# A two-block transformer kernel on one core: the transposed x is split piece by piece at the stage boundaries

## The reference, cut to what matters

```
x = x + 0.5 * swiglu(rmsnorm(x, g), w_in, w_out)     # eight of these, d_ff 2816
x = x + mixer(rmsnorm(x, g), ...)                     # hgrn, forgetting attention (fox), short conv, sparse attention (nsa)
kv = projection of rmsnorm(x, kv_norm)                # keys and values for nsa

rmsnorm(x, g) = x * rsqrt(mean(x*x) + 1e-6) * g
swiglu(h, w_in, w_out) = (silu(h @ w_in[gate]) * (h @ w_in[up])) @ w_out
```

## Time and profile before

| | us |
|---|---|
| median of 3 runs | 2198.05 |
| lowest, highest | 2197.47, 2202.11 |
| the profiled execution | 2199.34 |
| its span, first to last instruction | 2197.9 |
| TensorE busy | 2122.4 |
| VectorE busy | 1202.0 |
| ScalarE busy | 1009.3 |
| mean granted clock of TensorE | 0.988 |

### The profile page before, as it was taken

The page is one execution under the profiler, slowest core; times in us unless marked ns, Lnnn a source line. Parts: engine busy times, 40 slices in busy tenths (PEclk is TensorE's granted clock), DMA queues, the critical chain, the costliest instruction groups (busy, mean ns, idle before and its releaser), DMA issues.

```text
span 2197.9 us, 25948 instructions
## 1 busy us (share of the span) xinstructions
PE 2122.4 (97%) x10523; PEld 1756.2 (80%) x10523; DVE 1202.0 (55%) x1458; ACT 1009.3 (46%) x1272; POOL 25.6 (1%) x49
## 2 busy tenths in 40 slices
PE   8998999999999999999999999899999999998999
PEld 6887987888888776788888879788876887787887
DVE  6445686554545564654465556555555445765444
ACT  6344435444544454553454343444445344764342
POOL 1000000000000000000000000000000000000000
PEclk9999999999999999999999999999999999979999
DMA  8553425565555441455555535675635754213553
GB/s 262 192 172 116 153 96 173 194 204 194 196 173 194 132 154 58 144 194 196 174 173 192 196 129 175 188 225 172 199 107 127 236 173 156 98 39 133 193 173 115
DMA packets 265379, 361.01 MB, mean 164 GB/s; under 512 B 19856, under 2 KB 206652, under 8 KB 265133
## 3 DMA queue, kind: packets, MB, share of 16 engines
q1 hardware_dynamic: 256800, 351.57, 48.4%
q10 hardware_dynamic: 7772, 7.17, 1.9%
q0 software_dynamic: 688, 0.62, 0.1%
HBM read 357.75 MB, written 1.57 MB: 163 GB/s over the span
## 4 chain that ended last, share of the span: by engine, by line
PE 90%; DVE 6%; ACT 3%; issue 1%; ACTq 1%; DMA 0%; POOL 0%; SPq 0%; DVEq 0%
PE bank L388 18%; PE bank L390 17%; PE bank L389 17%; PE acc L648 6%; PE acc L649 6%; PE acc L650 6%; PE bank L383 2%; PE bank L385 2%; PE bank L384 2%; PE tr L628 2%; PE acc L678 1%; PE acc L680 1%; PE acc L679 1%; PE tr L471 1%; DVE x_tok L774 1%
## 5 line engine op out<-in xcount | busy, mean ns | idle before, releaser
L388 PE MATMUL bank<-w_hi_,xt_hi_ 128*128 128x512 f32 x1760 | 708.0, 402 | 12.1 <-DVE h_tok L753 4.9
L412 DVE TENSOR_TENSOR w_lo_<-raw_in,w_hi_ 128x2048 fp32r<-128x2048 f32 (+1 forms) x327 | 572.4, 1759 | 225.1 <-ACT w_hi_ L402 224.8
L390 PE MATMUL bank<-w_hi_,xt_lo_ 128*128 128x512 f32 x1760 | 689.3, 392 | 0.0
L389 PE MATMUL bank<-w_lo_,xt_hi_ 128*128 128x512 f32 x1760 | 687.9, 391 | 0.0
L402 ACT ACTIVATE w_hi_<-raw_in 128x2048 fp32r<-128x2048 f32 (+1 forms) x327 | 480.0, 1483 | 78.4 <-PE bank L390 22.8
L758 DVE TENSOR_TENSOR wo_lo_<-raw_out,wo_hi_ 128x2048 fp32r<-128x2048 f32 x80 | 183.4, 2292 | 478.8 <-ACT wo_hi_ L724 478.8
L388 PEld LDWEIGHTS bank<-w_hi_,xt_hi_ 128*128 128x128 f32 x1760 | 332.3, 189 | 82.6 <-issue 6.6
L390 PEld LDWEIGHTS bank<-w_hi_,xt_lo_ 128*128 128x128 f32 x1760 | 331.5, 188 | 71.5
L389 PEld LDWEIGHTS bank<-w_lo_,xt_hi_ 128*128 128x128 f32 x1760 | 332.7, 189 | 62.7
L724 ACT ACTIVATE wo_hi_<-raw_out 128x2048 fp32r<-128x2048 f32 x80 | 153.3, 1916 | 365.1 <-PE acc L650 358.0
L648 PE MATMUL acc<-wo_hi_,ht_hi_ 128*128 128x512 f32 x576 | 224.2, 389 | 0.0
(11 more groups left out here) (314 smaller groups left out, 1825.4 us busy)
## 6 DMA issues: line engine op xcount, KB each, us to landing
raw_in<-ffn_w_in SPq DMA_DIRECT2D x352, 512.0 KB, 4.9
raw_out<-ffn_w_out SPq DMA_DIRECT2D x88, 1024.0 KB, 4.9
raw_in<-hg_w_in SPq DMA_DIRECT2D x16, 1024.0 KB, 5.1
raw_in<-fox_w_in SPq DMA_DIRECT2D x16, 1024.0 KB, 5.4
raw_in<-conv_w_in SPq DMA_DIRECT2D x12, 1024.0 KB, 5.2
raw_in<-hg_w_out SPq DMA_DIRECT2D x4, 1024.0 KB, 5.0
raw_in<-fox_w_out SPq DMA_DIRECT2D x4, 1024.0 KB, 5.1
raw_in<-conv_w_out SPq DMA_DIRECT2D x4, 1024.0 KB, 5.2
```

The costliest lines, as they stand in the source:

```text
L388: mm(o, g.xt_hi_[:, k, tok], wh[:, par, k, 0:w], start=first, stop=False)
L389: mm(o, g.xt_hi_[:, k, tok], wl[:, par, k, 0:w], start=False, stop=False)
L390: last = mm(o, g.xt_lo_[:, k, tok], wh[:, par, k, 0:w], start=False, stop=end)
L412: dve.e.tensor_tensor(g.piece(g.wl, n, half, k), raw, g.piece(g.wh, n, half, k).bitcast(F32), ALU.subtract).then_inc(g.w_lo, 4 if k is Non ...
```

## The change

The turn of x is changed in all thirteen stages. The gains product into `g.xg` and the semaphore `scaled` are gone. ScalarE reads a 128x128 piece of the transposed x from PSUM and applies the gains as its scale; VectorE computes piece * gain - high part in one instruction, from the same piece in PSUM. Each stage has 16 such pieces on each engine in place of four halves (ScalarE) and four plus four (VectorE). Tile 1 is turned into banks of its own, two of the accumulators, and k alternates between the two banks of a tile. ScalarE waits for VectorE's piece k-2 before it reads piece k, so that the two never read one bank together. `xt_lo` and `xt_hi` now count pieces, and the product waits for each k. hgrn, conv and kv (`BY_K`) take the pieces in the order k, then tile; the others tile, then k. In mixer stages both diagonals are made before the first piece. In FFN stages the squares, the roots and 1/rms move from the turn of x to the `between` place of chunk 0.

The routines that turn other operands (`pe_turn_o` and its like) keep their instructions; only their counts change. Two waits are added in stages 8 and 10, where small matmuls use a bank that the turn of x now uses.

```diff
+BY_K = (S_HGRN, S_CONV, S_KV)
...
+def turn_order(s):
+    if s in BY_K:
+        return [(t, k) for k in range(KT) for t in range(NT)]
+    return [(t, k) for t in range(NT) for k in range(KT)]
...
+def pieces_for(u, t, k, feature_major, both):
+    if both:
+        return 8 * (k // 4) + 8
+    if u not in U:
+        return 8 * t + 4 * (k // 4) + 4
+    if U.index(u) in BY_K:
+        return 2 * k + (2 if feature_major else t + 1)
+    return 8 * (1 if feature_major else t) + k + 1
...
-            if f == 0 and k % 4 == 0:
-                operands(k // 4)
+            if f == 0:
+                operands(k)
...
+def x_turned(g, s, t, k):
+    a = 2 if s == S_FFN[7] else 0
+    bank = (g.tr[0], g.tr[1], g.accs[a], g.accs[a + 1])[2 * t + k % 2]
+    return bank[:, k // 2 * P:(k // 2 + 1) * P]
...
 def pe_turn_x(g, pe, s):
-            if t:
-                pe.wait_ge(g.scaled, 4 * s + half + 1)
             pe_wait_x(g, pe, s, t, half)
...
+def act_norm(g, act, s):
+    for t in range(NT):
+        act_squares(g, act, s, t)
+    for t in range(NT):
+        act_root(g, act, s, t)
...
 def act_turn_x(g, act, s, first=None):
...
+    if s in DIAG:
+        for t in range(NT):
             act_squares(g, act, s, t)
+            act_root(g, act, s, t)
+    act.wait_ge(g.prod, free)
+    for i, (t, k) in enumerate(turn_order(s)):
+        act.wait_ge(g.turned, 4 * turned_before(u) + 2 * t + 2)
+        if k >= 2:
+            act.wait_ge(g.xt_lo, 16 * u + turn_order(s).index((t, k - 2)) + 1)
+        act.e.activation(g.xt_hi_[:, k, t * P:(t + 1) * P], x_turned(g, s, t, k), ACT.Copy,
+                         scale=g.gains[:, GAIN[s] + k:GAIN[s] + k + 1]).then_inc(g.xt_hi, 1)
+        if first and (t, k) == (0, KT - 1):
             first()
...
+def dve_turn_x(g, dve, s, first=None):
...
+    for i, (t, k) in enumerate(turn_order(s)):
+        dve.wait_ge(g.xt_hi, 16 * u + i + 1)
+        place = g.xt_hi_[:, k, t * P:(t + 1) * P].bitcast(F32)
+        dve.e.scalar_tensor_tensor(g.xt_lo_[:, k, t * P:(t + 1) * P], x_turned(g, s, t, k),
+                                   g.gains[:, GAIN[s] + k:GAIN[s] + k + 1], place, ALU.mult,
+                                   ALU.subtract).then_inc(g.xt_lo, 1)
...
 # act_ffn, and in the same way dve_ffn with dve_norm
-                          between=(lambda: turn(c - 1)) if c else None)
+                          between=(lambda: turn(c - 1)) if c else (lambda: act_norm(g, act, s)))
```

More of the change, by code:

```diff
@@ L84 @@
 w_hi w_lo prod wo_hi wo_lo second acc narrow_mm
-turned scaled xt_hi xt_lo squares ms root rstd diag x_new
+turned xt_hi xt_lo squares ms root rstd diag x_new
 first_gains other_turned other_gains lb_e lower_bound
@@ L360, in pe_product, with operands @@
 def pe_product(g, pe, n, t, out, u, w=CW, feature_major=False, slot=None, both=False):
[L363 to L368, removed]
+    def operands(k):
+        pe.wait_ge(g.w_lo, 8 * n + 4 * (k // 4) + 4)
+        pe.wait_ge(g.xt_lo, 16 * u + pieces_for(u, t, k, feature_major, both))
     wh, wl, par = g.wh, g.wl, n % 2
@@ L521, in dve_ms, with dve_norm @@
     dve.e.reciprocal(g.rstd_[:, t:t + 1], g.sums[:, t, 3:4]).then_inc(g.rstd, 1)
-def dve_turn_x(g, dve, s, gain, first=None):
+def dve_norm(g, dve, s):
+    for t in range(NT):
+        dve_ms(g, dve, s, t)
+def dve_turn_x(g, dve, s, first=None):
     u = U[s]
[L527 to L530, removed]
     if s in DIAG:
[L533 to L552, removed]
         for t in range(NT):
             dve_ms(g, dve, s, t)
+            dve.wait_ge(g.rstd, 2 * s + t + 1)
+            dve.e.tensor_scalar(g.diag_[:, t, :], g.ident[:], g.rstd_[:, t:t + 1], None, ALU.mult).then_inc(g.diag, 1)
+    for i, (t, k) in enumerate(turn_order(s)):
[4 more added lines that the diff above has]
+                                   ALU.subtract).then_inc(g.xt_lo, 1)
+        if first and (t, k) == (0, KT - 1):
+            first()
 def pe_turn_o(g, pe, u, src, ready):
@@ L561, in pe_turn_o @@
             if t:
-                pe.wait_ge(g.xt_lo, 4 * u + half + 1)
+                pe.wait_ge(g.xt_lo, 16 * u + 4 * half + 4)
             pe.wait_ge(*ready(t))
@@ L580, in dve_turn_o @@
         for half in range(2):
-            dve.wait_ge(g.xt_hi, 4 * u + 2 * t + half + 1)
+            dve.wait_ge(g.xt_hi, 16 * u + 8 * t + 4 * half + 4)
             place = slice(4 * half, 4 * half + 4), slice(t * P, (t + 1) * P)
             dve.e.tensor_tensor(g.xt_lo_[:, place[0], place[1]], g.tr[half][:].rearrange("p (k n) -> p k n", k=4),
-                                g.xt_hi_[:, place[0], place[1]].bitcast(F32), ALU.subtract).then_inc(g.xt_lo, 1)
+                                g.xt_hi_[:, place[0], place[1]].bitcast(F32), ALU.subtract).then_inc(g.xt_lo, 4)
 def pe_out(g, pe, s, u, n, both=False):
@@ L740, in dve_ffn @@
     n0 = N0[s]
-    dve_turn_x(g, dve, s, FFN_GAIN[f], first)
+    dve_turn_x(g, dve, s, first)
     def turn(c):
@@ L1471, in pe_bias_slot @@
         pe.wait_ge(g.rel_in, 32)
+        pe.wait_ge(g.xt_lo, 16 * U[S_FFN[5]] + 16)
         pe.wait_ge(g.kv_set, 1)
@@ L1570, in pe_compress_slot @@
     if j == 4:
-        pe.wait_ge(g.scaled, 4 * S_FFN[6] + 4)
+        pe.wait_ge(g.xt_lo, 16 * U[S_FFN[6]] + KT)
         pe_kv_turn(g, pe, 3)
@@ L1927, in turn_o @@
             act.e.activation(g.xt_hi_[:, 4 * half:4 * half + 4, t * P:(t + 1) * P],
-                             banks[t][:].rearrange("p (k n) -> p k n", k=4), ACT.Copy).then_inc(g.xt_hi, 1)
+                             banks[t][:].rearrange("p (k n) -> p k n", k=4), ACT.Copy).then_inc(g.xt_hi, 4)
     def part(time, half):
@@ L2043, in turn_o @@
         for t in range(NT):
-            dve.wait_ge(g.xt_hi, 4 * U_NSA_O + 2 * half + t + 1)
+            dve.wait_ge(g.xt_hi, 16 * U_NSA_O + 8 * half + 4 * t + 4)
             place = slice(4 * half, 4 * half + 4), slice(t * P, (t + 1) * P)
             dve.e.tensor_tensor(g.xt_lo_[:, place[0], place[1]], banks[t][:].rearrange("p (k n) -> p k n", k=4),
-                                g.xt_hi_[:, place[0], place[1]].bitcast(F32), ALU.subtract).then_inc(g.xt_lo, 1)
+                                g.xt_hi_[:, place[0], place[1]].bitcast(F32), ALU.subtract).then_inc(g.xt_lo, 4)
     def part(time, half):
```

52 lines of the change are left out of this document (17 added, 35 removed).

## The result

The changed kernel took 2215.65 us, the median of 4 runs (2213.36 to 2218.53), against 2199.06 of the kernel before (4 runs, 2197.47 to 2202.11). The ratio is 1.007, 95% interval 1.0054 to 1.0085, so it is slower by 0.7%. Forecast were 2214 and a range of 2202 to 2227. The profiled execution has a span of 2213.4 us, 15.5 over that of before.

What follows compares the result with a forecast made beforehand. TensorE, busy 97% of the span, was taken as the bound, with ScalarE the long engine at FFN boundaries. FFN stages +20.4 and mixers -4.6 made +15.8, so 2215.1 profiled and 2214 as median, range 2202 to 2227.

Steps and rivals of the forecast that it cites:

- Start: Stage 2's FFN boundary: first product at about 370.5 against 371.60, 1.1 us gained; eight FFN boundaries have this start.
- Pieces: FFN turn of x: a ScalarE piece takes 0.34 us (bounds 0.26 and 0.40), spaced 0.375 (bounds 0.27 and 0.42).
- Chunk 1: Stage 2: TensorE waits 2.4 us before chunk 1, starting 1.3 later, and 0.9 at k=4; +2.3 in all.
- rival C: Clock falls in more places, at five boundaries with waits of 2.4 and 0.9: +1.3 each, 2220 us; chance 0.20.
- Stage 3: FFN boundary with three loads before the split: wait 4.1 us, half speed for 4.4 us; +5.2 (bounds 2.3 and 6).
- Stage 0: First FFN stage: 0.4 gained at the start, late half 1 weights, norm wait, extra table load; +4.7 (bounds 2 and 6).
- Stage 8: FFN boundary with six loads before the split: squares, roots and pieces uncovered; +4.3 (bounds 3 and 5).
- Stage 10 and kv: Stage 10: start 1.7 earlier, clock holds, norm hidden, -3.0 (bounds -1.5 and -3.3); kv with earlier diagonal; together -4.0.
- nsa: Mixer boundary: start gains 1.8 us as in fox, but pieces end 0.55 later than the copies; +0.6 (bounds -1 and +1).
- A: Before silu 0 of chunk 0: ScalarE's slack suffices, so only earlier starts count; 2181 us, near 17 less; chance 0.09.
- B: FFN pieces: cheaper, spaced 0.27 to 0.30 us, seven boundaries fall by 1.2 to 1.6; 2203 us; chance 0.20.
- D: Mixer boundaries: mixers win nothing, since k-by-k pieces starve the feature-major pass; 2219 us; chance 0.08.

Runs made afterwards that it cites:

- norm_back: The changed kernel with only the FFN norm put back in its old place: 2209.65 us, ratio 1.0039 to the kernel before.
- by_k: The changed kernel with the FFN pieces of all FFN stages but stage 0 ordered k, then tile, over four banks: 2207.27 us, ratio 1.0035 to the kernel before.
- tile1_halves: The changed kernel, but in FFN stages tile 1 goes by halves from its own banks and the norm is in its old place: 2198.99 us, ratio 0.9983.
- ffn_as_before: The changed kernel with the old turn and norm restored in FFN stages, new turn kept in the five mixer stages: 2198.96 us, ratio 0.9988.
- own_banks: ffn_as_before, with tile 1 of the FFN stages turned into banks of its own, still by halves: 2199.58 us, ratio 0.9997 to the kernel before.
- after_again: The changed kernel, unchanged, repeated for a second profile: 2216.74 us, ratio 1.007 to the kernel before.
- nsa_as_before: ffn_as_before with nsa's turn by halves too, but ScalarE squares tile 1 behind tile 0's copies, unlike the kernel before: 2201.21 us, ratio 1.0000.
- norm_moved_alone: The kernel before with only the FFN norm moved behind chunk 1's first split: 2205.74 us, ratio 1.0024 to the kernel before.
- before_again: The kernel before, unchanged, repeated for a second profile: one run of 2202.5 us.
- t1_halves_loads: tile1_halves with ScalarE's loads moved later: stage 3's three and stage 8's four weight transfers behind chunk 0, its tables behind tile 0's pieces: 2206.19 us, ratio 1.0025.

## Why the prediction was right

The sum, 15.8, met 15.6 and 17.2. The mechanism, ScalarE's queue ahead of silu 0, is shown by taking work out of it: the norm (norm_back), the exchange of pieces (by_k), tile 1's pieces (tile1_halves against norm_back, stage 2 from +1.6 to +0.3), and all of it (ffn_as_before).

*Start.* 1.1 forecast; 371.60 plus the lag of 1.92 is 373.52, and the product began at 372.53: 0.99. But I put it down to tile 1's transposes being free as well, and own_banks shows that this alone gives nothing. In stage 12 the start gained 1.7 (tile 1's transposes had waited 2.2 there), which I had not set apart; the stage lost 1.6, not 2.3.

*Pieces.* 0.34 forecast, 0.374 and 0.376 measured; 0.375 apart forecast, 0.395 measured. The Trainium skill (ScalarE: Activation LUTs, "What ACT_TABLE_LOAD costs") led to an estimated 0.386 and 0.395; the trace agrees with the spacing and lies 0.01 under the length. I took the nearest row over a page that counted the terms of just this form.

*Chunk 1.* Waits of 2.4 and 0.9 forecast; 1.73 and 0.67 measured. From 385.43 to 389.11 are 3.68 for four steps that take 2.74 at 0.686; 0.67 is the wait and 0.27 stands in no wait. Chunk 1 began 0.9 later than before (1.3 forecast) and lost 1.1 more inside (0.9 forecast). So a stage lost 2.0 by smaller waits than forecast and slower starts behind them; my own two terms make 2.2, and 2.3 went into the sum. Behind these waits the clock stayed at full speed in stages 2, 5 and 12 of both profiles, but not always. Stage 6, after:

```profile
1141.55 0.50 PE L408 MATMUL bank<-w_hi_,xt_hi_ 128*128 128x512 f32 x1 [1.83 <-DVE h_tok L767]
...
1143.24 0.63 PE L408 MATMUL bank<-w_hi_,xt_hi_ 128*128 128x512 f32 x1
```

Behind the wait of 1.83 matmuls take 0.63, the granted clock is 0.50 from 1142.80 to 1145.00, the second wait is gone, and the stage loses 2.7; in after_again the wait of 1.80 has full speed behind it and the stage loses 2.0. So rival C came about in one stage of one profile; why there and not elsewhere, the runs don't tell.

*Stage 3*, 5.2 forecast, 3.5 and 3.8 measured, is the term mis-sized most among the FFN stages. The loads overlap the last piece and cost 1.2 us, not 1.7, and the queue was 0.4 shorter as in stage 2, so the wait was 2.91, not 4.1; the lower clock behind it lasted less. Windows after, the start of chunk 1 in stages 2, 3 and 8 (columns as in the earlier trace rows):

```profile
385.40:389.10 3.70, 3.01 (x12) 2.17 (x12) 2.34 (x2) 3.70 (x4) 0.00 (x0) 1.00 0.27 94
576.60:581.00 4.40, 4.40 (x13) 3.57 (x14) 3.07 (x3) 4.40 (x4) 0.00 (x0) 0.66 0.24 83
1443.40:1448.00 4.60, 4.60 (x14) 3.67 (x15) 2.89 (x5) 4.29 (x7) 0.00 (x0) 0.65 0.75 85
```

0.34 of 4.4 us is 1.5 lost, where I had 2.2.

*Stage 0*, 4.7 forecast, 4.3 and 3.8 measured: TensorE waits 1.54 for w_lo in chunk 0 (1.3 forecast), 2.01 for h (2.4 forecast) and 1.17 for w_lo in chunk 1.

*Stage 8*, 4.3 forecast, 3.3 and 3.7 measured. The wait for h is 7.21 against 4.91, and that for the table c_rel 1.33 against 0.36. But this stage lost about 2 even with FFN turns as before. In ffn_as_before ScalarE's six issues last 10.5 us, from 1412.87, against 9.4 in the kernel before, and the table is waited for 1.3 us instead of 0.4. Behind that wait, in ffn_as_before:

```profile
1416.02 1.03 PE L1540 MATMUL acc<-arena 33*16 33x512 f32 x2 [1.29 <-DMA arena<-c_rel]
...
1417.94 0.63 PE L412 MATMUL bank<-w_hi_,xt_lo_ 128*128 128x512 f32 x1
```

Matmuls take 0.63 there and 0.40 at the same place in the kernel before; in the changed kernel they fall to 0.63 too (from 1429.67). nsa_as_before lost 2.0 with the same wait (1.37) and no such fall, but waited 5.4 for h in place of 3.6. What of the changed mixers or of the added wait in this stage sets this off isn't shown.

*Stage 10 and kv*, -4.0 forecast, -2.1 and -1.5 measured. The start came as forecast (over kv and the first chunk of stage 10 the lag fell from 12.8 to 8.3). Half of it was given back in chunk 2, behind a late weight transfer:

```profile
1726.14 1.92 ACT L422 ACTIVATE w_hi_<-raw_in 128x2048 fp32r<-128x2048 f32 x1 [6.93 <-DMA raw_in<-ffn_w_in]
```

TensorE waits 2.6 for ht_lo behind it. Counted from the close of stage 8, this transfer was issued 4.6 us earlier than before (at 86.8 for 91.4) and landed only 2.1 earlier (106.1 for 108.2), which is the gain that was left. That step was missing from my sum.

*Mixers.* hgrn, fox and conv at -2.4, -1.5 and -1.3 (-3.7, -1.4 and +0.3 in after_again) for -2.3, -0.9 and -1.0.

*nsa*, 0.6 forecast, 3.2 and 4.5 measured: its product starts 1.8 sooner, then TensorE waits 2.0 for the normed q, and at that point (1898.72) the stage is 0.4 behind the kernel before, as I had it. The kernel before has no wait there. In six of the nine profiles with the new turn matmuls of 0.63 us follow it, and in four of these the stage is 2.4 to 2.7 behind soon after, after_again among them. The rest arises later, at the lower clock. The same stretch, from 76 to 88 us behind the start of nsa, after and before:

```profile
1954.00:1966.00 12.00, 12.00 (x53) 11.21 (x54) 8.23 (x30) 7.01 (x17) 0.84 (x1) 0.50 0.07 25
```

```profile
1943.27:1955.27 12.00, 10.82 (x69) 10.00 (x68) 9.32 (x32) 7.96 (x19) 0.83 (x1) 0.78 0.18 60
```

At 0.50, the 1.2 GHz level, TensorE is busy all of the time with 53 matmuls; in the kernel before it gets 69 done. Where such a fall lands differs from profile to profile of one kernel. With the new turn nsa came out between -0.2 and +6.9 (nine profiles, mean 3.5), with the old one at 0, +0.7 and +2.2 (before, norm_moved_alone, before_again; mean 1.0). Whether the new turn costs these 2.5 us on average or the clock wandered is open, with three profiles on one side.

So the total is right partly by luck: stages 0, 3, 8 and 12 were forecast 0.4 to 1.7 too high, 3.8 together; against that stood nsa, forecast 2.6 too low, and kv with stage 10, forecast 1.9 too low. Of the other rivals, A is out (TensorE does wait for h), B is out (0.395 apart), and D is out (hgrn and fox gain in every kernel that has their new turn).

## What to carry to other kernels

A tuned kernel's slack can sit on an engine that is 46% busy: count, in order, what it must do between the start of a stage and the first release the bound engine needs, and charge each edit's work against it once. Cutting a tile into pieces helps for the pieces that the next product waits for, and costs on the rest; and when two engines hand pieces back and forth, give them enough banks that neither waits for the other. Restoring an old part for an experiment restores the order on every engine, or it tests something else (nsa_as_before). Before moving a transfer, see what small transfer it then runs ahead of.

## What the runs showed of the hardware

- The same scaled 128x128 activation out of PSUM issued every 0.25 us over four banks (by_k) and every 0.395 over two (the changed kernel), though one lasts 0.37 to 0.48.
- The same wait of 2.29 us in conv was followed by full speed in one profile of the changed kernel and by matmuls of 0.63 us in place of 0.39 in the other. conv came out at -1.3 and +0.3. Equal waits of 2.17 (stage 12 of the kernel before) and of 1.83 and 1.80 (stage 6 of the changed one) were parted in the same way. The second of conv's (after_again):

```profile
1394.77 0.47 PE L408 MATMUL bank<-w_hi_,xt_hi_ 128*128 128x512 f32 x1 [2.29 <-DVE xt_lo_ L865]
...
1395.71 0.63 PE L408 MATMUL bank<-w_hi_,xt_hi_ 128*128 128x512 f32 x1
```

- A single stage of unchanged code (nsa) wandered by 2.2 us between two profiles of one kernel, and by 7 among nine profiles with the same turn of it. A difference of a few us in one profile's nsa says nothing; stages 2 and 5 can be read to 0.1.
- ScalarE's issue of the same 32 KB transfer took 5.76 us (stage 8 of tile1_halves) or 9.87 (t1_halves_loads), at another place in ScalarE's program.
